# Queries of an attention mixer turned by VectorE and moved by DMA in place of TensorE's transposes

## What is computed

```python
q, k, v, gate = split(h @ w_in)                      # 2048, 256, 256, 2048 columns
q, k = rms_norm(q, q_gain), rms_norm(k, k_gain)      # per head
s = einsum('qhd,kd->hqk', q_group, k_group) * 64 ** -0.5 + bias   # this block and the one before
m = max(max(s), sink)
p = exp(s - m);  p = p / (sum(p) + exp(sink - m))
o = einsum('hqk,kd->qhd', p, v_group)
x = x + (o * silu(gate)) @ w_out
```

## Time and profile before

| | us |
|---|---|
| median of 3 runs | 1422.65 (1422.07 to 1422.69) |
| the profiled execution | 1422.24 |
| its span, first to last instruction | 1420.5 |
| TensorE busy | 1414.2 (100%) |
| VectorE busy | 895.6 (63%) |
| ACT busy | 690.6 (49%) |
| GpSimd busy | 79.5 (6%) |
| stretch of the attention's units 0 to 8 | about 1100 to 1320 |

### The profile page before, as it was taken

One profiled execution on the slowest core, in us unless ns is written; L12 is line 12 of the kernel. 1 busy time (PEld: TensorE's weight loads), 2 busy tenths in 40 slices (PEclk: granted clock), 3 DMA queues, 4 the chain that ended last, 5 costly groups with the idle time before them and its releaser, 6 DMA issues.

```text
span 1420.5 us, 17662 instructions
## 1 busy us (share of the span) xinstructions
PE 1414.2 (100%) x6391; PEld 1161.4 (82%) x6391; DVE 895.6 (63%) x1133; ACT 690.6 (49%) x918; POOL 79.5 (6%) x64
## 2 busy tenths in 40 slices
PE   9999999999999999999999999999999999999999
PEld 7888888888888888888888888888888887777887
DVE  5599976765555555455555445556767759896653
ACT  7444555554444433444444344345556647666442
POOL 2000010000000000000000000000000134330000
PEclk9999999999999999999999999999999999999999
DMA  9765556776766656666666666667778687889752
GB/s 331 229 188 171 178 193 232 239 239 193 232 223 224 222 193 193 193 221 222 206 214 217 193 192 222 196 230 235 239 237 274 205 279 244 262 272 296 251 198 89
DMA packets 169575, 314.93 MB, mean 222 GB/s; under 512 B 11713, under 2 KB 33981, under 8 KB 169384
## 3 DMA queue, kind: packets, MB, share of 16 engines
q1 hardware_dynamic: 154632, 282.22, 61.0%
q10 hardware_dynamic: 13088, 25.18, 5.7%
q0 software_dynamic: 1792, 6.71, 1.4%
HBM read 291.47 MB, written 22.59 MB: 221 GB/s over the span
## 4 chain that ended last, share of the span: by engine, by line
PE 97%; DMA 1%; DVE 1%; ACT 1%; issue 0%; POOL 0%; SPq 0%; ACTq 0%
PE acc L1478 31%; PE acc L1479 31%; PE acc L1480 31%; PE acc L1540 1%; PE sp L1691 1%; PE tp L1707 1%; PE tp L1498 1%; DVE w_lo L955 0%; DMA parked<-wide 0%; DMA wide<-parked 0%; DMA w_raw<-in_w_in 0%; ACT w_hi L629 0%; POOL rs L565 0%; PE sp L1618 0%; PE sp L1530 0%
## 5 line engine op out<-in xcount | busy, mean ns | idle before, releaser
L955 DVE TENSOR_TENSOR w_lo<-w_raw,w_hi 128x1024 fp32r<-128x1024 f32 x488 | 598.7, 1230 | 478.1 <-ACT w_hi L629 476.4
L629 ACT ACTIVATE w_hi<-w_raw 128x1024 fp32r<-128x1024 f32 x500 | 528.4, 1060 | 659.1 <-PE acc L1480 655.3
L1478 PE MATMUL acc<-w_lo,yh 128*128 128x512 f32 x1056 | 411.5, 390 | 0.0
L1480 PE MATMUL acc<-w_hi,yl 128*128 128x512 f32 x1056 | 410.9, 389 | 0.0
L1479 PE MATMUL acc<-w_hi,yh 128*128 128x512 f32 x1056 | 410.8, 389 | 0.0
L1478 PE MATMUL acc<-w_lo,hh 128*128 128x512 f32 x784 | 307.5, 392 | 0.0
L1480 PE MATMUL acc<-w_hi,hl 128*128 128x512 f32 x784 | 305.2, 389 | 0.0
L1479 PE MATMUL acc<-w_hi,hh 128*128 128x512 f32 x784 | 305.2, 389 | 0.0
L1478 PEld LDWEIGHTS acc<-w_lo,yh 128*128 128x128 f32 x1056 | 198.3, 188 | 41.8 <-issue 0.6
L1480 PEld LDWEIGHTS acc<-w_hi,yl 128*128 128x128 f32 x1056 | 198.3, 188 | 41.2
L1479 PEld LDWEIGHTS acc<-w_hi,yh 128*128 128x128 f32 x1056 | 198.3, 188 | 40.7
(11 more groups left out here) (163 smaller groups left out, 661.4 us busy)
## 6 DMA issues: line engine op xcount, KB each, us to landing
w_raw<-in_w_gate SPq DMA_DIRECT2D x88, 512.0 KB, 4.4
w_raw<-in_w_up SPq DMA_DIRECT2D x88, 512.0 KB, 4.3
w_raw<-in_w_down SPq DMA_DIRECT2D x88, 512.0 KB, 3.6
w_raw<-in_w_in SPq DMA_DIRECT2D x64, 512.0 KB, 4.3
w_raw<-in_swa_w_in ACTq DMA_DIRECT2D x48, 512.0 KB, 5.4
w_raw<-in_w_out SPq DMA_DIRECT2D x32, 512.0 KB, 4.2
w_raw<-in_w_ple_gate SPq DMA_DIRECT2D x32, 512.0 KB, 5.5
w_raw<-in_swa_w_out SPq DMA_DIRECT2D x32, 512.0 KB, 4.2
```

The source lines that it names most:

```text
L629: act.activation(w_hi[:, s % SPL], w_raw[:, s % RAW], ACT.Copy).then_inc(hi_ready, 1)
L955: dve.tensor_tensor(w_lo[:, s % SPL], w_raw[:, s % RAW], w_hi[:, s % SPL].bitcast(F32), ALU.subtract).then_inc(lo_ready, 1)
L1478: pe.matmul(dst, xh[:, f, tk], w_lo[:, s % SPL, k], start=(f == 0), stop=False)
L1480: last = pe.matmul(dst, xl[:, f, tk], w_hi[:, s % SPL, k], start=False, stop=(f == CK * n - 1))
```

## The change

The 32 transposes of queries on TensorE and the eight copies from PSUM on ACT go. After ACT's `take`, at (v, 3), VectorE turns the queries in blocks of 32x32 into a buffer of its own, `q_blocked` (`turn_queries`); SP puts it to a scratch `parked_q` and fetches it back into the same buffer (`put_queries`, `fetch_queries`); ACT copies it, scaled, to `tile[4]` (`queries_in_place`), at the place where the copy from PSUM was. TensorE's `score(g, 0)` waits for that. In SP's list groups 0 and 1 stand between the keys and the first probabilities; the put of groups 2 and 3 stands ahead of the put of probabilities 2 and 5, its fetches ahead of theirs. The fourth buffer of probabilities is now `tile[7]`, which was free in this stage. The halves of PSUM are renumbered (`H_PV`).

```diff
@@ -87,15 +87,12 @@
 H_SWA = len(HALVES)
 HALVES += "xx"
 
-H_Q, H_PV = {}, {}
-for _v in range(2, 9):
+H_PV = {}
+for _v in range(4, 9):
     if _v >= 5:
         H_PV[_v - 5, 2] = len(HALVES); HALVES += "a"
-    if 4 <= _v <= 7:
+    if _v <= 7:
         H_PV[_v - 4, 0] = len(HALVES); HALVES += "a"
-    if _v <= 5:
-        H_Q[_v - 2] = len(HALVES); HALVES += "aa"
-    if 4 <= _v <= 7:
         H_PV[_v - 4, 1] = len(HALVES); HALVES += "a"
 
 T_FFN, T_HID, T_PLE, T_SWA, T_K, T_OG = 0, 4, 15, 19, 22, 23
@@ -166,6 +163,7 @@
     x_v = x.rearrange("b (t p) n -> p (b t) n", p=P)
     out_v = out.rearrange("b (t p) n -> p (b t) n", p=P)
     parked = nc.dram_tensor("parked", (P, 1024), F32, kind="Internal").ap()
+    parked_q = nc.dram_tensor("parked_q", (P, 1024), F32, kind="Internal").ap()
     parked_p = [nc.dram_tensor(f"parked_p{i}", (P, 1024), F32, kind="Internal").ap() for i in range(4)]
 
     with ExitStack() as ctx:
@@ -189,13 +187,15 @@
             third_bias = second.enter_context(nc.sbuf_tensor("third_bias", [P, D], F32))
             prob = [second.enter_context(nc.sbuf_tensor(f"prob{i}", [P, 1024], F32)) for i in range(2)]
             other_bias = second.enter_context(nc.sbuf_tensor("other_bias", [P, D], F32))
-            prob += [second.enter_context(nc.sbuf_tensor(f"prob{i}", [P, 1024], F32)) for i in range(2, 4)]
+            prob.append(second.enter_context(nc.sbuf_tensor("prob2", [P, 1024], F32)))
+            q_blocked = second.enter_context(nc.sbuf_tensor("q_blocked", [P, 1024], F32))
         oh, ol = sb("oh", [P, KT, S], F32R), sb("ol", [P, KT, S], F32R)
         hh, hl = sb("hh", [P, KT, S], F32R), sb("hl", [P, KT, S], F32R)
         resid = sb("resid", [P, T, D])
         wide = sb("wide", [P, T, D])
         big = sb("big", [P, D])
         tile = [sb(f"tile{i}", [P, 1024]) for i in range(8)]
+        prob.append(tile[7])
 
         def tok(i):
             return tile[i][:].rearrange("p (t n) -> p t n", t=T)
@@ -287,6 +287,10 @@
         p_blocks = sem("p_blocks")
         p_out = [sem(f"p_out{i}") for i in range(4)]
         p_in = [sem(f"p_in{i}") for i in range(4)]
+        q_blocks = sem("q_blocks")
+        q_out = sem("q_out")
+        q_in = sem("q_in")
+        q_ready = sem("q_ready")
         blocks_out = sem("blocks_out")
         turned_hi = sem("turned_hi")
         turned_lo = sem("turned_lo")
@@ -426,6 +430,16 @@
                 sp_.wait_ge(blocks_out, 16 * (n + 1) + 16 * lap.turns)
                 from_quarters(turn_buffers(n)[1], parked, turned)
 
+            def put_queries(g):
+
+                sp_.wait_ge(q_blocks, g + 1)
+                sp_.dma_start(parked_q[:, :], q_blocked[:]).then_inc(q_out, 16)
+
+            def fetch_queries(g):
+
+                sp_.wait_ge(q_out, 16 * (g + 1))
+                from_quarters(q_blocked, parked_q, q_in)
+
             def put_probs(n):
 
                 sp_.wait_ge(p_blocks, n + 1)
@@ -505,9 +519,19 @@
 
             put(T_K)
             fetch(T_K)
-            for n in range(9):
-                put_probs(n)
-                fetch_probs(n)
+            for g in range(2):
+                put_queries(g)
+                fetch_queries(g)
+            for g in range(3):
+                for n in (3 * g, 3 * g + 1):
+                    put_probs(n)
+                    fetch_probs(n)
+                if g < 2:
+                    put_queries(g + 2)
+                put_probs(3 * g + 2)
+                if g < 2:
+                    fetch_queries(g + 2)
+                fetch_probs(3 * g + 2)
             put_probs(9)
             put(T_OG)
             fetch_probs(9)
@@ -870,6 +894,16 @@
                 src = tp[h % 2][:, 0:HD * nh].rearrange("p (q k n) -> p k q n", q=4, n=32)
                 act.activation(dst.rearrange("p k (q n) -> p k q n", q=4), src, ACT.Copy).then_inc(tp_left["a"], 1)
 
+            def queries_in_place(g):
+
+                act.wait_ge(q_in, 64 * (g + 1))
+                if g:
+                    act.wait_ge(scores, 3 * g)
+                src = q_blocked[:].rearrange("p (q k t n) -> p k t q n", q=4, k=4, t=T)
+                for t in range(T):
+                    last = act.activation(quarters(feat(4))[:, :, t], src[:, :, t], ACT.Copy, scale=gqk[:, 0:1])
+                last.then_inc(q_ready, 1)
+
             def og_high(g):
 
                 act.wait_ge(og_ready, g + 1)
@@ -902,12 +936,13 @@
                     if (v, c) == (2, 6):
                         keys()
                     if c == 1 and 3 <= v <= 6:
-                        copy(H_Q[v - 3], tile[4], gqk[:, 0:1])
+                        queries_in_place(v - 3)
                     if c == 2 and 4 <= v <= 7:
                         exp(v - 4, 2)
                     if c == 3 and 2 <= v <= 5:
                         if v > 2:
                             act.wait_ge(q_squares, v - 2)
+                            act.wait_ge(q_blocks, v - 2)
                         take(SWA_UNIT + v - 1, tok(1), ACT.Copy, rr)
                     if c == 3 and v >= 6:
                         if v > 6:
@@ -1300,6 +1335,16 @@
                 dve.tensor_reduce(ms[:, R_Q + g, :], tile[5][:].rearrange("p (h n) -> p h n", n=HD), AX,
                                   ALU.add).then_inc(want, 1)
 
+            def turn_queries(g):
+
+                wait_left(dve, SWA_UNIT + 1 + g)
+                if g:
+                    dve.wait_ge(q_ready, g)
+                into = q_blocked[:].rearrange("p (r k t n) -> p k r t n", r=4, k=4, t=T)
+                for t in range(T):
+                    last = dve.transpose(into[:, :, :, t], tok(1)[:, t].rearrange("p (k r n) -> p k r n", k=4, r=4))
+                last.then_inc(q_blocks, 1)
+
             def turn_probs(g, r):
 
                 n = 3 * g + r
@@ -1427,6 +1472,8 @@
                         scale_gate(v - 6)
                     if c == 3 and v >= 7:
                         gated(v - 7)
+                    if c == 3 and 2 <= v <= 5:
+                        turn_queries(v - 2)
                     if c == 4 and 4 <= v <= 7:
                         turn_probs(v - 4, 2)
                         denominators(v - 4, 2)
@@ -1683,7 +1730,7 @@
                 if n == 0:
                     pe.wait_ge(turned_hi, T_K + 1)
                 if r == 0:
-                    wait_half_left(pe, H_Q[g] + 1)
+                    pe.wait_ge(q_ready, g + 1)
                 w = P * nk
                 for i in range(nh):
                     h = h0 + i
@@ -1727,9 +1774,6 @@
                         weigh(v - 4, 0)
                     if c == 4 and 3 <= v <= 6:
                         score(v - 3, 2)
-                    if c == 4 and 2 <= v <= 5:
-                        wait_left(pe, u - 1)
-                        to_features(H_Q[v - 2], tok(1))
                     if c == 6 and 2 <= v <= 5:
                         score(v - 2, 0)
                     if c == 6 and 4 <= v <= 7:
```

## The result

The changed kernel takes 1426.28 us (median of 11 runs, 1424.75 to 1428.74) beside 1421.87 us for the kernel before (11 runs on the same chip, 1421.57 to 1422.69). The ratio is 1.0031, interval 1.0023 to 1.0040: it is slower, by 4.4 us. The profiled execution took 1428.04 us with a span of 1426.3 us, against 1422.24 and 1420.5, so it shows 5.8 us. Of these, 0.87 us lie ahead of the stage (SP's put of the keys goes out at 1148.99 here and at 1148.12 before, with nothing of the change ahead of it); the rest is in the attention stage. This execution is 1.8 us above the median, so the terms read from its trace add up to 5.8 us and not to 4.4.

A forecast was written before the change was run, and what follows sets the result against it. TensorE was taken as the bound, busy 1414.2 of 1420.5 us. Group shifts of +2.3, -0.85, (-0.85 + 0.85) and (-0.85 + 1.1) gave +1.7 us on the 1422.65 median: 1424.3 us, range 1420.6 to 1429.0.

The forecast's parts named there:

- The likeliest case: Whole kernel: time stays within 0.2% (2.85 us) of the kernel before, 1419.8 to 1425.5 us; chance 0.62.
- puts of 8.4 us: SP's queue between groups 2 and 3: put landing time used for the range's upper end, 1429.0 us.
- What TensorE saves: TensorE's query transposes: 0.85 us saved per group, 3.4 us for four; with the 0.4 us wait, at most 3.8.
- Group 0: First queries: put after keys' fetches lands in 5.0 us, ready at 1168.3, wait about 3.6 us, shift +2.3.
- The sum: Attention stage: savings and new waits on TensorE add microsecond for microsecond to +1.7 us; median 1424.3 us.
- Groups 2 and 3: Later queries, through SP's full queue: TensorE waits 0.85 us in group 2 and 1.1 us in group 3.
- Rival (b): SP's queue chain between groups 2 and 3: slow put landings make the kernel slower, 1427.1 us; chance 0.30.
- the point of slower: SP's queue: with four puts landing in 7.6 us each, shift reaches +2.85 us, the limit for slower.
- 1221.85 + 4x: SP's queue: time group 3's queries are ready if four puts each land in x, against TensorE's 1249.40.
- (a) Quiet transfers: Query transfers: puts land in 3.5 us, fetches in 6.0, shift -2.05 us, time 1420.6 us; chance 0.12.
- (c) Intervals not won: TensorE's transpose intervals: scores beside them take the slot, nothing won after group 0, +2.3 us, 1425.0; chance 0.03.
- (d) VectorE as the bound: VectorE: load rises from 91 to 96%, low parts late to TensorE, some 2 us, 1426.3 us; chance 0.05.

The follow-up runs named there:

- e_none: Changed kernel with queries neither turned nor moved, ACT copying its own tile (wrong operand): 1419.39 us, ratio 0.9982 to the kernel before.
- e_unheeded: Changed kernel doing all turning and moving, but ACT copies its own tile and nobody waits (wrong operand): 1419.75 us, ratio 0.9985.
- e_before_bias: Kernel before with only the third bias load moved behind the first low parts: 1421.61 us, ratio 0.9998.
- e_g0pe: Changed kernel with group 0 transposed by TensorE as before, groups 1 to 3 by VectorE and DMA: 1420.07 us, ratio 0.9991.
- e_fill18: Changed kernel with 18 filling products of 128x128 on TensorE ahead of its wait for the first queries: 1427.79 us, ratio 1.0046.
- e_early_bias: Changed kernel with the first queries' put ahead of the keys' fetches and the third bias load behind the first low parts: 1424.86 us, ratio 1.0019.
- e_g0only: Kernel before with only group 0 turned by VectorE and moved by DMA: 1428.81 us, ratio 1.0051.
- e_early: Changed kernel with the first queries' put moved ahead of the keys' fetches in SP's list: 1424.61 us, ratio 1.0018.
- e_early_keys: As e_early, with ACT putting the keys in place three chunks later: 1424.36 us, ratio 1.0017 to the kernel before.
- e_fill: Changed kernel with 36 filling products of 128x128 on TensorE ahead of its wait for the first queries: 1427.93 us, ratio 1.0044.

## Why the prediction was right or wrong

**The total.** 1424.3 was forecast, 1426.28 measured, inside the range of 1420.6 to 1429.0. The likeliest case, no difference above 0.2%, was wrong: the change is slower by 0.31%. The mechanism of the forecast (the gain is given back at the queries' landings) was right for the first group; terms of its sum were mis-sized and one was missing. (The upper end of the range, puts of 8.4 us, is 1428.7 by the forecast's own formula; this changes nothing.)

**What TensorE saves.** The interval of 0.85 us for eight transposes was right (0.75 to 0.85 us in groups 1 to 3). "If the queries come in time that is won too: 3.8 us is the most that can be gained" was too high: with the work left out altogether the gain is 2.3 us by the medians and 2.9 to 3.0 bunch against bunch. I took the 0.4 us wait for something behind the transposes. It was the end of another chain, keys, three splits, copies, which let the first scores start at 1164.9 in e_none, 1166.0 before and 1166.4 in e_unheeded, 5.3 to 5.4 us behind the keys each time; in e_before_bias the keys came 2.7 us earlier and the wait was gone. How much of the first group's share can be won depends on when the keys land: 1.0 us in e_none's trace.

**Group 0.** The step that carried the forecast. The order in the queue and the time of the put (1155.86 against 1155.8) were right. The landing of 5.0 us, chosen because ACT has no weights on order, was 6.7 us, beyond my upper bound of 5.9. The engines were full (share 1.00 and 1.02 between 1156 and 1160, at 169 and 286 GB/s): the keys' own fetches, issued just ahead, were still on the way, and so was a weight chunk that ACT had ordered at 1154.78, before it stopped. Fetch to ACT took 6.6 us, not 6.25, and the copies 1.3 us, not 1.25. The queries were ready at 1170.5, not 1168.3, and the wait was 5.1 us, not 3.6.

**The missing term.** The sum treats an idle microsecond of TensorE as one microsecond. After 5.1 us of it the granted clock stood at 0.50, and 2.7 us more were lost. This is the largest single error. On the forecast's basis for the profiled execution, the first scores 2.4 us later than forecast and the clock give 1423.9 + 2.4 + 2.7 = 1429.0; measured are 1428.04, and the 1.0 us between is the next point. The median is 1.8 us lower than this execution, and no trace tells which term is smaller in it.

**Groups 2 and 3.** A wait of 0.85 us in group 2 was forecast and none showed; 1.1 us in group 3, and 0.82 showed. That is near by luck, since the steps were wrong. Group 2's put went out at 1207.47, where I had 1207.2, but only because TensorE was 6.5 us later than before and not 1.45, and the second probabilities' put landed in 4.8 us and not 8.9. Its own landing took 9.4 us, where I took 6.6. The error behind this is that I kept the queue's times of the kernel before. The queue follows TensorE: the first probabilities' put goes at 1191.73 instead of 1184.52, 7.2 us later, much as the scores they come from (1182.82 instead of 1175.44). So it is not true that the queries of group 2 come at a fixed time. In six of the eight traces in which they go this way and are waited for, ACT's copies end 26.4 to 26.9 us behind the start of group 1's scores, and TensorE takes 26.8 us from these to group 2's: there is no slack, and the wait is 0 to 0.3 us, whether group 0 was late (the changed kernel) or not (e_g0pe). In the other two the copies end after 28.1 us (e_fill18) and 29.8 (e_early_bias), with the slowest fetch at 8.2 and 8.1 us against 5.6 to 6.7 in the six, and TensorE waits 1.44 and 3.18 us.

**Rival (b), slower by SP's queue.** It had 0.30 and 1427.1 us, near the measured time, and its landings came: the four puts from group 2 to group 3 were seen landed after 9.4, 9.3, 6.3 and 4.7 us, mean 7.4, where it put the point of slower at 7.6. But they are not the cause. In e_g0pe the same four took 9.1, 9.6, 6.2 and 4.4 us, mean 7.3, and that kernel waits 0.3 us in all and is not slower than the one before. The formula 1221.85 + 4x starts from a fixed time, and the chain starts where TensorE lets it. Group 0 is enough alone (e_g0only, +7.0 us); that (b) named nearly the right time is luck. From group 3's first fetch to ACT's copies it was 9.2 us, against 6.4 taken.

The Trainium skill (DMA: Bandwidth & Descriptors, "Anatomy of one DMA — SWDGE (gpsimd) path") would have 3.2 us for such a put of 512 KB, an estimate by its formula, which is for another path. That is near the 3.5 us of e_before_bias, and a third to two thirds of the 4.7 to 9.4 us in the full stretches here. The choice of the rows over that figure was right, and the rows were still too low.

**The other rivals.** (a) Quiet transfers: no, by the same landings. (c) Intervals not won: no, 0.75 to 0.85 us each. (d) VectorE as the bound: its busy time rose from 69.1 to 72.0 of 76 us, and e_unheeded, with all of that load, loses 0.4 us against e_none, within the noise. The DMA share rose from 0.82 to 0.97 where "an eighth" gave 0.92.

**What the rule on transposes said.** The Trainium skill (VectorE: DVE Perf Modes, "Rules for kernel authors") leaves the full 128x128 transpose to TensorE. For the first group the measurement agrees (+7.0 us without it). For the others it does not: groups 1 to 3 without TensorE are 1.7 us faster by the medians, with an interval that touches no change. What decides here is when the result is wanted, not the price of the transpose.

## What to carry to other kernels

Before work is taken off the critical engine, ask what else ends at the same moment as its result: the removal is worth only the distance to that second chain, and a kernel with the work left out measures it (2.3 to 3.0 us here, not 3.8). A put, wait and fetch through one queue costs its round trip (13.3 us from the first put to ACT's copy) from the moment when the queue is free, so the first use, for which the queue is not free in time, should keep the old way, and the later ones may take the new, with nothing to spare (two of eight traces waited 1.4 and 3.2 us in group 2): e_g0pe, at 1420.07 us the fastest kernel here that computes the reference, though its interval touches no change. Price a stall of TensorE with its clock behind it. Time a serial queue from the event that feeds it, not from the clock time it had before: when the bound engine moves, the queue moves with it, and what decides is whether its round trip fits between two of that engine's own steps.

## What the runs showed of the hardware

- The granted clock after idle time: 5.11 us idle, then 0.50 for some 7 us, 2.7 us lost; 6.09 us idle, 1.7 us lost. It fell after 3.12 us idle in one kernel and after 3.18 in another, and did not after 3.20 in a third, nor after 2.83 behind a fill. Two nearly equal waits can differ by 2.9 us in the end (9.48 us to the second scores in e_early, 12.42 in e_early_keys). The four kernels with a wait of 2.8 to 5.1 us before the first scores spread over 4 to 7 us, the kernel before over 1.1 to 1.5; with 6.09 us of wait, where the clock fell in all five runs, the spread is 1.8.
- A put of 512 KB by SP took from 3.1 us (e_fill, probabilities at 1199.38) to 10.6 us (e_early, at 1242.27) to its landing; 9.1 us stood beside 4.8 for the same put of probabilities in two kernels. Of the four fetches of group 2's queries (128 KB each) the slowest took 5.6 to 8.2 us in eight traces.
- A product of 128x128 with the identity in fp32 took 0.228 us, in two records each; a transpose of the same size takes 0.11 us from start to start.
- Queries fetched while ACT ordered weights landed later (slowest fetch 9.8 us in e_early_keys) than in e_early (6.6), where ACT stood for the keys; but with ACT standing in e_early_bias it was 9.4, so ACT's orders are not shown to be the reason.
